# The entry of the feed-forward stages: order of the weight split, the norm's parts and the first tiles

## The chip, the cores and the metric

The kernel runs on one core of one Trainium2 chip. The metric is the device time of one execution, in microseconds (us), as the median of three. The core has TensorE (PE, matmuls; PEld is its weight load), VectorE (DVE), ScalarE (ACT), GpSimd (POOL) and SyncE (SP), which issues most of the transfers. Each engine works through its own list of instructions in program order and waits on semaphores for the others.

## The reference

A block of mixed attention, memory attention and a mixture of experts (two layers) is followed by a second block of two layers, where the change lies. In a layer `l` of the second block, tokens `x` (512 x 1024) and, in layer 0 only, a context `cx` (256 x 1024) go through a mixer and then through a feed-forward stage:

```
h2 = modulate(rms_norm_2(x, norm2_g[l]), sh2, sc2)     # h * (1 + sc2) + sh2
x  = x + g2 * sq_relu_mlp(h2, w_ff1[l], w_ff2[l])      # square(relu(h2 @ w1)) @ w2
# layer 0 only, with the context's own shift, scale and gate:
cx = cx + cg2 * sq_relu_mlp(hc2, w_ff1[l], w_ff2[l])   # w1 1024 x 4096, w2 4096 x 1024
```

Everything is float32.

## The kernel before

Tensors lie transposed: 1024 features as KD = 8 blocks of 128 partitions, tokens along the free dimension, 512 (T) tokens and 256 (CT) of the context side by side. `both` is true in layer 0, where the context is computed too.

**Products in three parts.** In the feed-forward stage a float32 product is made of three faster ones: each operand is split into a rounded high part and the rest, a low part, and high x high + high x low + low x high are summed in one PSUM bank. `tile3` (L713) does that for one output tile of 128 features: for each k of 8 it issues high x high, high x low, low x high, 24 matmuls, waiting for `needs[k]` if given. `joint3` (L687) does it for several tiles at once: all products with the high part of the tokens first (two passes over k, each k of the first waiting for its `needs_high`), then all with the low part (waiting for `needs_low`). It was used so far in the mixer and memory stages of the first block. Banks come from a ring of six (PB).

**Weights.** A block is 1 MB (128 x 2048 values), loaded by SyncE in a fixed order into slots. `split_high` (L1547, ScalarE) waits for the load and rounds the block to its high part, one activation; `split_low` (L2168, VectorE) waits for that and subtracts, one operation. TensorE's `weight_parts` waits for the latter. `ff_chunks` (L388) gives the order of the blocks: ff1 (slab 0, half 0), ff1 (0, 1), ff1 (1, 0), ff1 (1, 1), ff2 (0, 0), and so on. A block of ff1 holds two output tiles, m = 2i and 2i + 1.

**Entry of the stage.** At the end of the mixer stands the differential attention: `df_units(l)` lists its units (16 in layer 1; 24 in layer 0, of which the last four, as four in the middle, are of the context). For each unit ScalarE does two exps and, later, a copy of the turned result; VectorE does two maxima (`df_top`) and one join (`df_join`); TensorE scores, turns and multiplies with the values. A last group of the output projection and the sums of the norm's squares follow on TensorE. Then the engines meet (`meet(("ff", l))`), and:

- ScalarE (L2022 on): `high(0)`, the first block's split; the norm's root (a logarithm and an exp) for the tokens and, in layer 0, the context; `mod_shift` (L1794): the high parts ("hh") of the eight token blocks, then of the context's, each with the shift added.
- VectorE (L2701 on): `low(0)`; `mod_norm` (L2452): for the tokens three Newton steps on the root, then scaled tokens ("h", k) and low parts ("h2", k - 2) in turn; then the same for the context. A high part needs its scaled token, a low part needs its high part.
- TensorE (L1436): for block 0 tile m = 0 of the tokens, the same tile of the context, then m = 1 of both; then the next block.

Then a loop over the blocks: at step n ScalarE first splits block n + 1, then takes the two tiles of block n: relu of the tokens' bank, relu of the context's bank, square of both, rounded copy (hidden, high part). VectorE makes the low part of block n + 1 and then the low parts of the hidden tiles. With `both`, the next layer's conditioning (ada) blocks come between the blocks from step 3 on.

Of the kernel before, what the change touches and what calls it, by code (L numbers as in the profile page):

```python
# [29 lines left out]
ADD, MUL, SUB, MAX = ALU.add, ALU.mult, ALU.subtract, ALU.max  # L30
# [177 lines left out]
class Steps:  # L208
# [9 lines left out]
    def after(self, key):  # L218

        sem, value = self.known[key] if self.known is not None else ("tensor_step", 1)  # L220
        return self.sems[sem], value
# [61 lines left out]
def build(nc, A, known):  # L283

    ctx = ExitStack()
    with ctx:
# [382 lines left out]
        def _(eng):  # L669
# [530 lines left out]
            for l in range(L):  # L1200
# [227 lines left out]
                for n, (kind, s, i) in enumerate(ff_chunks()):  # L1428
                    a = n - 1 - ADA_AT
                    if l == 0 and 0 <= a < 3 * KD:  # L1430
                        ada(1, a // KD, a % KD, PO)
                    if l == 0 and a >= KD + 1 and (a - 1) % KD == 0 and a <= 3 * KD + 1:
                        ada_turn(1, (a - 1) // KD - 1, PO)
                    key = (kind, l, s, i)
                    wh, wl = weight_parts(key)
                    if kind == "ff1":  # L1436
                        for m in range(2 * i, 2 * i + 2):
                            c = slice(P * (m % 2), P * (m % 2) + P)
                            for part, cols, N, tag in parts:
                                tile3(("f1" + part, l, s, m), [(wh[:, k, c], wl[:, k, c]) for k in range(KD)],  # L1440
                                      [(S["HH"][:, k, cols], S["HL"][:, k, cols]) for k in range(KD)], N,
                                      free=(WF(key),) if m % 2 and part == parts[-1][0] else (),
                                      needs=[("h2", (tag, l), k) for k in range(KD)] if (s, m) == (0, 0) else ())
                    else:
                        hid = S["HID"].get((l, s))
                        for m in range(4 * i, 4 * i + 4):
                            c = slice(P * (m % 4), P * (m % 4) + P)
                            for part, cols, N, tag in parts:
                                end = part == parts[-1][0] and m % 4 == 3
                                tile3(("f2" + part, l, s, m), [(wh[:, k, c], wl[:, k, c]) for k in range(4)],  # L1450
                                      [(hid[:, k, cols], hid[:, 4 + k, cols]) for k in range(4)], N,
                                      free=((WF(key),) if end else ()) + ((S["HID"].free((l, s)),) if end and i else ()),
                                      needs=[("hid", l, s, k) for k in range(4)] if m == 0 else ())
                            if s == SLABS - 1 and m >= 2:
                                next_sums([m - 2])
# [5 lines left out]
        def _(eng):  # L1461
# [105 lines left out]
            for l in range(L):  # L1567
# [7 lines left out]
                def high(t):  # L1575
                    eng.wait_ge(*after(("rope", l, t)))
                    act(S["H5R"][:, t, :], S["TA"].get(("g", l, t))).then_inc(*done(("high5", l, t)))
# [235 lines left out]
            for l in range(L):  # L1813
# [174 lines left out]
                def df_roots(j):  # L1988
                    root(("od", l, j), S, PB)
                    if both:  # L1990
                        root(("odc", l, j), S, PB, CT)
# [8 lines left out]
                for i in range(len(us) + DF_LAG + 1):  # L2000
                    if i == len(us) // 2 + DF_POST - 1:
                        df_squares(0)
                    if i == len(us) // 2 + DF_POST:
                        df_roots(0)
                    if i < len(us):
                        df_exp(us[i], 0)
                    if DF_LAG <= i < len(us) + DF_LAG:
                        df_down(us[i - DF_LAG])
                    if i < len(us):
                        df_exp(us[i], 1)  # L2010
                    if DF_LAG < i and df_ends(us[i - DF_LAG - 1]):
                        u = us[i - DF_LAG - 1]
                        shares(df_okey(u), S, u[3] + 1)
# [8 lines left out]
                    split_high((kind, l, s, i))  # L2022

                order = list(ff_chunks())
                high(0)
                root(("n2x", l), S)
                if both:
                    root(("n2c", l), S, n=CT)
# [36 lines left out]
        def _(eng):  # L2065
# [117 lines left out]
            for l in range(L):  # L2183
# [30 lines left out]
                def low(t):  # L2214
                    eng.wait_ge(*after(("high5", l, t)))
                    tt(S["L5R"][:, t, :], S["TA"].get(("g", l, t)), S["H5R"][:, t, :], SUB).then_inc(*done(("low", l, t), S["TA"].free(("g", l, t))))
# [235 lines left out]
            def mod_norm(n, l, S, H, both, parts=None):  # L2452

                for r in range(2 if both else 1):
                    tag = (f"n{n}{'xc'[r]}", l)
                    N = (T, CT)[r]
                    cols = slice(0, T) if r == 0 else slice(T, T + CT)
                    y = rstd(tag, S, PO, N)
                    for k in range(KD + 2):
                        if k < KD:  # L2460
                            stt(H[:, k, cols], (X, C)[r][:, k, :], (G1, G2)[n - 1][l][:, k, r:r + 1], y, MUL, MUL).then_inc(*done(("h", tag, k), *((S["Y"].free(tag),) if k == KD - 1 else ())))
                        if parts and k >= 2:
                            eng.wait_ge(*after(("hh", tag, k - 2)))
                            stt(parts["HL"][:, k - 2, cols], H[:, k - 2, cols], ADA[l][:, 22 + k, r:r + 1], parts["HH"][:, k - 2, cols], ADD, SUB).then_inc(*done(("h2", tag, k - 2)))

            def ada_columns(l, q, ring):
                key = ("adT", l, q)
# [12 lines left out]
            for l in range(L):  # L2480
# [136 lines left out]
                def beside(g):  # L2617
                    return lambda i: add_out(g, range(2 * i - 2, 2 * i)) if 1 <= i <= KD // 2 else None
# [58 lines left out]
                us = df_units(l)  # L2677
                for i in range(len(us) + DF_LAG + 2):
                    beside(1)(i)
                    if i < len(us):  # L2680
                        df_top(us[i], 0)
                    if 1 <= i <= len(us):
                        u = us[i - 1]
                        df_join(u)
                        if df_ends(u):
                            shares(df_okey(u), S, [])
                    if i == len(us) // 2 + DF_POST:
                        df_post(0)
                    if i < len(us):
                        df_top(us[i], 1)  # L2690
                    if DF_LAG + 1 < i and df_ends(us[i - DF_LAG - 2]):
                        u = us[i - DF_LAG - 2]
                        c = int(u[0] == "dc")
                        out_scaled(df_okey(u), S, (T, CT)[c], S["YG"][:, u[2], (slice(0, T), slice(T, T + CT))[c]], ("od2", l, u[2], c))
# [8 lines left out]
                    split_low((kind, l, s, i))  # L2703

                order = list(ff_chunks())
                low(0)
                mod_norm(2, l, S, S["H"], both, S)
                for n, (kind, s, i) in enumerate(order):
                    a = n - 2 - ADA_AT
# [214 lines left out]
```

## Time and profile before

| | us |
|---|---|
| median of 3 runs | 3247.66 (3245.68 to 3249.27) |
| profiled execution | 3246.96 |
| its span, first to last instruction | 3245.3 |
| TensorE busy | 3011.3 |
| VectorE busy | 1348.9 |
| ScalarE busy | 1088.3 |
| mean granted clock of TensorE | 0.970 |

The span is what the timeline covers; times in the rows count from its start. Layer 0's feed-forward stage begins near 1893 us, layer 1's near 2870 us, and the latter runs almost to the end. A row of the timeline gives the start, the duration, engine and line, what is written and read, how many instructions are merged ("x3") and, in brackets, how long the engine had stood before and which engine ended it. "PEclk" is the granted clock of TensorE, 1.00 for 2.4 GHz, 0.50 for 1.2 GHz.

### The profile page before, as it was taken

The numbers are of one execution on the slowest core, as the hardware profiler recorded it, in microseconds if no ns is written. First come the engines' busy times: TensorE is split into PE (matmuls) and PEld (weight loads), VectorE is DVE, ScalarE is ACT, GpSimd is POOL, SyncE is SP. The second block draws the span as 40 slices with busy tenths as digits, with TensorE's granted clock in tenths as the row PEclk, the third lists the DMA queues.
The fourth block names the chain that finished last, engine by engine and source line by source line (L and its number), as shares of the span: only waits on it lengthen the run. The fifth ranks groups of instructions, "written<-read, shape, count | busy, mean of one in ns | idle before, by whom it ended". The sixth has DMA issues, their size and how long they took to land.

```text
span 3245.3 us, 39893 instructions
## 1 busy us (share of the span) xinstructions
PE 3011.3 (93%) x16068; PEld 2129.5 (66%) x16068; DVE 1348.9 (42%) x2127; ACT 1088.3 (34%) x1869; POOL 248.5 (8%) x334
## 2 busy tenths in 40 slices
PE   7999979979999799989999789999999999879998
PEld 5657855446568754446676558887886576658886
DVE  5665432246655422334234653232333341644434
ACT  4555321134654311142122542222222131543332
POOL 0011010000100200010002210000001001200000
PEclk9999989999999899999999989999999999989999
DMA  3011259951013299953211002322321221012221
GB/s 145 27 40 69 89 204 415 417 228 52 14 47 111 91 400 418 415 226 142 79 53 39 1 34 110 125 109 104 130 80 58 105 78 46 14 52 91 104 91 52
DMA packets 61492, 414.20 MB, mean 128 GB/s; under 512 B 6992, under 2 KB 7504, under 8 KB 13696
## 3 DMA queue, kind: packets, MB, share of 16 engines
q1 hardware_dynamic: 55664, 392.59, 30.8%
q0 software_dynamic: 4496, 16.98, 1.6%
q8 instruction: 130, 2.13, 0.3%
q10 hardware_dynamic: 1152, 2.10, 0.2%
q14 instruction: 50, 0.41, 0.0%
HBM read 409.53 MB, written 2.10 MB: 127 GB/s over the span
## 4 chain that ended last, share of the span: by engine, by line
PE 85%; DVE 7%; DMA 3%; ACT 3%; issue 2%; POOL 1%; DVEq 0%; SPq 0%; ACTq 0%; POOLq 0%
PE banks L726 82%; PE banks L727 3%; DVE arena L2068 3%; DMA weight<-in_w_up 3%; ACT arena L1464 2%; DVE arena L2655 1%; DVE weight_part L2172 0%; DVE arena L2347 0%; DVE tokens_low L2068 0%; DVE x L2068 0%; DVE arena L2345 0%; POOL arena L2761 0%; ACT weight_part L1464 0%; DMA mats<-in_k_mats 0%; DVE arena L2119 0%
## 5 line engine op out<-in xcount | busy, mean ns | idle before, releaser
L1464 ACT ACTIVATE arena<-banks 128x512 f32<-128x512 f32 (+4 forms) x528 | 293.5, 560 | 1188.6 <-PE banks L726 1036.8
L726 PE MATMUL banks<-weight,arena 128*64 128x512 f32 (+5 forms) x2808 | 574.4, 527 | 27.1 <-ACT arena L1464 13.0
L726 PEld LDWEIGHTS banks<-weight,arena 128*64 128x64 f32 (+2 forms) x2808 | 268.6, 145 | 296.6 <-issue 262.0
L726 PE MATMUL banks<-hidden,weight_part 128*128 128x512 f32 (+1 forms) x2304 | 446.4, 355 | 0.0
L726 PE MATMUL banks<-arena,weight 128*128 128x512 f32 (+1 forms) x1120 | 422.7, 533 | 20.9 <-DVE arena L2068 10.7
L726 PE MATMUL banks<-tokens_high,weight_part 128*128 128x512 f32 (+1 forms) x1536 | 419.8, 359 | 22.9 <-DVE tokens_low L2068 22.8
L726 PEld LDWEIGHTS banks<-hidden,weight_part 128*128 128x128 f32 x2304 | 381.0, 189 | 70.3 <-issue 3.5
L726 PEld LDWEIGHTS banks<-arena,weight 128*128 128x128 f32 x1120 | 211.3, 193 | 212.5 <-issue 186.0
L726 PEld LDWEIGHTS banks<-tokens_high,weight_part 128*128 128x128 f32 x1536 | 275.7, 191 | 82.1 <-DVE tokens_low L2068 29.5
L726 PE MATMUL banks<-tokens_low,weight_part 128*128 128x512 f32 (+1 forms) x768 | 274.1, 357 | 0.0
L2172 DVE TENSOR_TENSOR weight_part<-weight,weight_part 128x2048 fp32r<-128x2048 f32 x98 | 225.1, 2300 | 86.7 <-ACT weight_part L1464 86.5
L1464 ACT ACTIVATE weight_part<-weight 128x2048 fp32r<-128x2048 f32 x98 | 186.0, 1908 | 172.3 <-DMA weight<-in_w_ff 115.5
L2068 DVE SCALAR_TENSOR_TENSOR x<-banks,arena,x 128x512 f32<-128x512 f32 x192 | 143.4, 750 | 232.7 <-PE banks L726 232.1
L2761 POOL TENSOR_TENSOR arena<-arena 128x512 f32<-128x512 f32 x72 | 87.2, 1212 | 1912.6 <-ACT arena L1464 1641.0
L726 PE MATMUL banks<-arena 128*64 128x128 f32 (+2 forms) x2176 | 223.7, 304 | 8.2 <-DVE arena L2129 2.6
L1464 ACT ACTIVATE arena<-banks,arena 128x512 f32<-128x512 f32 (+2 forms) x264 | 182.5, 696 | 129.2 <-DVE arena L2655 99.1
L727 PE MATMUL banks<-mats,arena 128*128 128x128 f32 x1168 | 170.2, 280 | 52.2 <-ACT arena L1464 23.5
L727 PEld LDWEIGHTS banks<-mats,arena 128*128 128x128 f32 x1168 | 133.1, 143 | 101.8 <-issue 45.2
L2719 DVE TENSOR_TENSOR hidden<-arena,hidden 128x768 fp32r<-128x768 f32 (+1 forms) x64 | 52.8, 826 | 332.8 <-ACT hidden L1464 332.8
L726 PEld LDWEIGHTS banks<-arena 128*64 128x64 f32 (+2 forms) x2176 | 149.1, 146 | 55.7 <-issue 35.0
L1464 ACT ACTIVATE arena<-arena 128x512 f32<-128x512 f32 (+5 forms) x270 | 164.8, 625 | 36.8 <-DVE arena L2068 11.7
L2068 DVE SCALAR_TENSOR_TENSOR arena<-arena 128x512 f32<-128x512 f32 (+7 forms) x223 | 121.1, 552 | 119.8 <-ACT arena L1464 109.8
(198 smaller groups left out, 3208.1 us busy)
## 6 DMA issues: line engine op xcount, KB each, us to landing
weight<-in_w_gate SPq DMA_DIRECT2D x64, 1024.0 KB, 13.6
weight<-in_w_up SPq DMA_DIRECT2D x64, 1024.0 KB, 8.2
weight<-in_w_down SPq DMA_DIRECT2D x64, 1024.0 KB, 10.8
weight<-in_w_ff SPq DMA_DIRECT2D x64, 1024.0 KB, 4.8
weight<-in_ada_w SPq DMA_DIRECT2D x48, 1024.0 KB, 5.1
weight<-in_w_in SPq DMA_DIRECT2D x28, 1024.0 KB, 7.6
weight<-in_w_o SPq DMA_DIRECT2D x8, 1024.0 KB, 4.8
weight<-in_w_mem_kv SPq DMA_DIRECT2D x8, 1024.0 KB, 4.8
```

The source lines that it names most:

```text
L726: mm = lambda o, a, b, first=True, last=True: eng.matmul(o, a, b, start=first, stop=last, skip_group_check=True)
L727: tr = lambda o, a, rows=P: eng.transpose(o, a, mat("ident", rows, rows))
L1464: act = lambda o, i, f=ACT.Copy, **k: eng.activation(o, i, f, **k)
L2068: stt = lambda o, a, s, b, p, q: eng.scalar_tensor_tensor(out=o, in0=a, scalar=s, in1=b, op0=p, op1=q)
L2172: tt(low, raw_of(key), high, SUB).then_inc(*done(("split", key)))
L2655: eng.tensor_reduce(s[:, half:half + 1], PB.get_pair(key)[:, 0:T + CT if u[0] == "d" else CT], AX, MAX, negate=True).then_inc(*done(("nb", ...
L2719: tt(hid[:, 4 + m, 0:N], t[:, 0:N], hid[:, m, 0:N], SUB).then_inc(*done(("hid", l, s, m), S["RT"].free((l, s, m))))
L2761: eng.tensor_tensor(a, a, S["SQ"].get((tag, k))[:, 0:n], ADD).then_inc(*done(S["SQ"].free((tag, k)), *((("summed", tag),) if k == first - ...
```

## The change

Four edits, the first three in both layers:

- `split_high` and `split_low` of the first block stand in the attention's loop: ScalarE's ahead of the last unit's first exp, VectorE's one step later, ahead of the last unit's join. `high(0)` and `low(0)` go.
- `mod_norm` makes all eight scaled tokens first and then all eight low parts, for the tokens and then for the context.
- TensorE takes the first block's two token tiles in one `joint3`.
- In layer 0 the token tiles of the second block come next, then the context's tiles of the first block (a `joint3`), then the context's tiles of the second.

```diff
--- before.py
+++ after.py
@@ -1433,14 +1433,28 @@
                         ada_turn(1, (a - 1) // KD - 1, PO)
                     key = (kind, l, s, i)
                     wh, wl = weight_parts(key)
-                    if kind == "ff1":
+                    if kind == "ff1" and s == 0:
+                        XP, CP = [[(S["HH"][:, k, cols], S["HL"][:, k, cols]) for k in range(KD)] for cols in (slice(0, T), slice(T, T + CT))]
+                        ms = range(2 * i, 2 * i + 2)
+                        if i == 0:
+                            first = wh, wl
+                            joint3([("f1", l, 0, m) for m in ms], [halves(first, m) for m in ms], XP, [range(KD)], T, [("hh", ("n2x", l), k) for k in range(KD)],
+                                   [("h2", ("n2x", l), k) for k in range(KD)], [(), () if both else (WF(key),)])
+                            continue
+                        for m in ms:
+                            tile3(("f1", l, 0, m), halves((wh, wl), m % 2), XP, free=(WF(key),) if m % 2 and not both else ())
+                        if both:
+                            joint3([("f1c", l, 0, m) for m in range(2)], [halves(first, m) for m in range(2)], CP, [range(KD)], CT, [("hh", ("n2c", l), k) for k in range(KD)],
+                                   [("h2", ("n2c", l), k) for k in range(KD)], [(), (WF(("ff1", l, 0, 0)),)])
+                            for m in ms:
+                                tile3(("f1c", l, 0, m), halves((wh, wl), m % 2), CP, CT, free=(WF(key),) if m % 2 else ())
+                    elif kind == "ff1":
                         for m in range(2 * i, 2 * i + 2):
                             c = slice(P * (m % 2), P * (m % 2) + P)
                             for part, cols, N, tag in parts:
                                 tile3(("f1" + part, l, s, m), [(wh[:, k, c], wl[:, k, c]) for k in range(KD)],
                                       [(S["HH"][:, k, cols], S["HL"][:, k, cols]) for k in range(KD)], N,
-                                      free=(WF(key),) if m % 2 and part == parts[-1][0] else (),
-                                      needs=[("h2", (tag, l), k) for k in range(KD)] if (s, m) == (0, 0) else ())
+                                      free=(WF(key),) if m % 2 and part == parts[-1][0] else ())
                     else:
                         hid = S["HID"].get((l, s))
                         for m in range(4 * i, 4 * i + 4):
@@ -2002,6 +2016,8 @@
                         df_squares(0)
                     if i == len(us) // 2 + DF_POST:
                         df_roots(0)
+                    if i == len(us) - 1:
+                        split_high(("ff1", l, 0, 0))
                     if i < len(us):
                         df_exp(us[i], 0)
                     if DF_LAG <= i < len(us) + DF_LAG:
@@ -2022,7 +2038,6 @@
                     split_high((kind, l, s, i))
 
                 order = list(ff_chunks())
-                high(0)
                 root(("n2x", l), S)
                 if both:
                     root(("n2c", l), S, n=CT)
@@ -2456,12 +2471,11 @@
                     N = (T, CT)[r]
                     cols = slice(0, T) if r == 0 else slice(T, T + CT)
                     y = rstd(tag, S, PO, N)
-                    for k in range(KD + 2):
-                        if k < KD:
-                            stt(H[:, k, cols], (X, C)[r][:, k, :], (G1, G2)[n - 1][l][:, k, r:r + 1], y, MUL, MUL).then_inc(*done(("h", tag, k), *((S["Y"].free(tag),) if k == KD - 1 else ())))
-                        if parts and k >= 2:
-                            eng.wait_ge(*after(("hh", tag, k - 2)))
-                            stt(parts["HL"][:, k - 2, cols], H[:, k - 2, cols], ADA[l][:, 22 + k, r:r + 1], parts["HH"][:, k - 2, cols], ADD, SUB).then_inc(*done(("h2", tag, k - 2)))
+                    for k in range(KD):
+                        stt(H[:, k, cols], (X, C)[r][:, k, :], (G1, G2)[n - 1][l][:, k, r:r + 1], y, MUL, MUL).then_inc(*done(("h", tag, k), *((S["Y"].free(tag),) if k == KD - 1 else ())))
+                    for k in range(KD if parts else 0):
+                        eng.wait_ge(*after(("hh", tag, k)))
+                        stt(parts["HL"][:, k, cols], H[:, k, cols], ADA[l][:, 24 + k, r:r + 1], parts["HH"][:, k, cols], ADD, SUB).then_inc(*done(("h2", tag, k)))
 
             def ada_columns(l, q, ring):
                 key = ("adT", l, q)
@@ -2677,6 +2691,8 @@
                 us = df_units(l)
                 for i in range(len(us) + DF_LAG + 2):
                     beside(1)(i)
+                    if i == len(us):
+                        split_low(("ff1", l, 0, 0))
                     if i < len(us):
                         df_top(us[i], 0)
                     if 1 <= i <= len(us):
@@ -2703,7 +2719,6 @@
                     split_low((kind, l, s, i))
 
                 order = list(ff_chunks())
-                low(0)
                 mod_norm(2, l, S, S["H"], both, S)
                 for n, (kind, s, i) in enumerate(order):
                     a = n - 2 - ADA_AT
```

## Rows read from the trace of the kernel before

**Rows 1.** The page's first part: engine, busy us, share of the span, instructions.

```profile
PE 3011.3 (93%) x16068; PEld 2129.5 (66%) x16068; DVE 1348.9 (42%) x2127; ACT 1088.3 (34%) x1869; POOL 248.5 (8%) x334
```

**Rows 2.** Waits of TensorE: us in total, times, longest.

```profile
PE banks L726 <- DVE tokens_low L2068: 22.8, 11, 9.3
```

**Rows 3.** Timeline, feed-forward entry, layer 0: start, us, engine, line, [idle <-releaser].

```profile
1893.45 1.91 ACT L1464 ACTIVATE weight_part<-weight 128x2048 fp32r<-128x2048 f32 x1 [1.64 <-PE banks L726]
...
1895.27 0.67 ACT L1464 ACTIVATE arena<-banks,vec 128x512 f32<-128x512 f32 x1
...
1895.97 0.63 ACT L1464 ACTIVATE arena<-arena 128x512 f32<-128x512 f32 x1
...
1897.70 0.68 DVE L2068 SCALAR_TENSOR_TENSOR arena<-arena 128x512 f32<-128x512 f32 x1
...
1899.87 2.08 DVE L2068 SCALAR_TENSOR_TENSOR arena<-x,arena 128x512 f32<-128x512 f32 x3
...
1900.72 1.99 ACT L1464 ACTIVATE tokens_high<-arena 128x512 fp32r<-128x512 f32 x3 [3.16 <-DVE arena L2068]
...
1902.76 0.77 PE L726 MATMUL banks<-tokens_high,weight_part 128*128 128x512 f32 x1 [9.34 <-DVE tokens_low L2068]
...
1919.47 2.29 DVE L2172 TENSOR_TENSOR weight_part<-weight,weight_part 128x2048 fp32r<-128x2048 f32 x1 [1.20 <-ACT weight_part L1464]
```

**Rows 4.** Same entry: stretch, us, busy PE PEld DVE ACT POOL, PEclk, DMA, GB/s.

```profile
1902.70:1906.50 3.80, 3.74 (x9) 2.51 (x9) 3.80 (x6) 1.99 (x4) 0.00 (x0) 0.50 0.02 4
...
1911.60:1913.60 2.00, 0.05 (x1) 0.00 (x0) 1.96 (x6) 1.23 (x3) 0.00 (x0) 1.00 0.00 0
...
1924.30:1927.10 2.80, 2.80 (x25) 2.80 (x24) 0.00 (x0) 0.60 (x1) 0.00 (x0) 1.00 0.00 0
...
1927.10:1943.80 16.70, 16.70 (x98) 14.78 (x97) 4.21 (x3) 7.16 (x9) 0.00 (x0) 1.00 0.18 64
```

**Rows 5.** Timeline, feed-forward entry of layer 1.

```profile
2869.94 1.91 ACT L1464 ACTIVATE weight_part<-weight 128x2048 fp32r<-128x2048 f32 x1 [1.76 <-PE banks L726]
...
2879.25 0.76 PE L726 MATMUL banks<-tokens_high,weight_part 128*128 128x512 f32 x1 [9.35 <-DVE tokens_low L2068]
...
2893.61 0.60 ACT L1464 ACTIVATE arena<-banks 128x512 f32<-128x512 f32 x1 [3.51 <-PE banks L726]
```

**Rows 6.** Timeline, end of differential attention, layer 0.

```profile
1853.93 0.47 ACT L1464 ACTIVATE arena<-banks,arena 128x256 f32<-128x256 f32 x1 [0.41 <-DVE arena L2655]
...
1855.78 0.16 DVE L2661 RECIPROCAL arena<-arena 128x1 f32<-128x1 f32 x1
...
1856.78 0.44 PE L727 MATMUL banks<-mats,arena 128*128 128x128 f32 x2 [0.95 <-DVE arena L2068]
```

**Rows 7.** Timeline, end of differential attention, layer 1.

```profile
2831.26 0.90 ACT L1464 ACTIVATE arena<-banks,arena 128x768 f32<-128x768 f32 x1 [2.49 <-DVE arena L2655]
...
2834.53 0.16 DVE L2661 RECIPROCAL arena<-arena 128x1 f32<-128x1 f32 x1 [1.06 <-ACT arena L1464]
...
2836.05 0.87 PE L727 MATMUL banks<-mats,arena 128*128 128x128 f32 x6 [1.07 <-DVE arena L2068]
```

**Rows 8.** Timeline, last part of the joint pass of the first stage.

```profile
37.46 3.79 PE L726 MATMUL banks<-mix_low,weight_part 128*128 128x512 f32 x16
```

**Rows 9.** Timeline, ScalarE and VectorE inside a block of layer 0.

```profile
1927.39 0.39 ACT L1464 ACTIVATE arena<-banks 128x256 f32<-128x256 f32 x1 [2.33 <-PE banks L726]
...
1929.44 1.90 ACT L1464 ACTIVATE weight_part<-weight 128x2048 fp32r<-128x2048 f32 x1
```

**Rows 10.** Stretches around two gaps of layer 1's attention and output projection.

```profile
2821.50:2824.50 3.00, 0.03 (x1) 0.00 (x0) 2.86 (x7) 1.97 (x4) 0.00 (x0) 1.00 0.03 5
...
2824.70:2828.00 3.30, 3.30 (x18) 2.67 (x20) 2.08 (x3) 0.23 (x1) 0.00 (x0) 0.50 0.00 0
...
2850.10:2855.30 5.20, 5.18 (x6) 2.17 (x7) 0.75 (x1) 0.56 (x1) 0.00 (x0) 0.50 0.00 0
```

**Rows 11.** Timeline of SyncE's queue, layer 1's first feed-forward block.

```profile
2705.73 0.33 SPq L665 DMA_DIRECT2D weight<-in_w_ff  x1
```

## The prediction

> **What bounds the kernel now.** I read the page's head first. TensorE is busy 93% of the span [rows 1], so only a gap on TensorE, or a stretch in which its clock is low, can give time back. The waits of TensorE come next: its waits for the feed-forward low parts are 22.8 us in 11 places, the longest 9.3 [rows 2]. They all lie in the two entries, so I read the timeline there, first layer [rows 3] and second [rows 5], the stretches of the first with clock [rows 4], and last the end of the attention, where the split is put [rows 6, 7].
>
> Entry of layer 0 [rows 3]: TensorE ends the sums at 1893.4; ScalarE splits the block (1.91 us) and only then takes the root; VectorE makes the block's low part (2.29 us, as that of the second block at 1919.47), then the Newton steps from 1897.70, the first scaled token from 1899.87; TensorE starts at 1902.76, after 9.34 us. From 1897.70 to 1918.27 VectorE works through tokens and context without a gap (20.57 us; the row at 1919.47 shows it idle for 1.20 before). Layer 1 is the same with tokens only [rows 5]: first matmul 2879.25.
>
> **Step 1, the split ahead of the norm.** The root now starts where the split started, at 1893.45. Its two activations take 1.33 us (1895.27 to 1895.97 + 0.63), VectorE follows 0.11 later as between these engines elsewhere, so Newton starts at 1894.89 instead of 1897.70: -2.8 us. What is late next is this chain itself, root, Newton, first token. The order is the same in layer 1, again -2.8. The weight block is there long before: in layer 1 its transfer is issued at 2705.7, 125 us ahead of the attention's last unit [rows 11].
>
> What it costs where it goes. Layer 1: ScalarE is idle for 2.49 us ahead of the last unit's first exp [rows 7], which hides 1.91. VectorE's part is put ahead of the last unit's join: VectorE is free 1.06 us before that join, at 2833.47, so the part runs to 2835.7, the join starts there instead of at 2834.53, and TensorE at 2836.05 waits for the join. +1.15 us. Layer 0: the last units are of the context and small, ScalarE is free only from 1853.5; its split runs to 1855.4 and holds up the exps behind it by 1.5 us at most. VectorE's low part takes the join's place, about 1855.7 to 1857.9; the join was at 1855.78, and TensorE at 1856.78 waits for it [rows 6]. +2.1 us. Behind this join everything up to the output projection is one chain, so both prices are paid in full. Bounds: 0, if another wait covers it, and 2.3, the whole instruction.
>
> **Step 2, scaled tokens ahead of low parts, joint passes.** (Times here and in steps 3 and 4 are without the attention's 2.1 and 1.15.) The first high part starts 0.85 us behind the first scaled token (1900.72 against 1899.87, [rows 3]) and takes 0.72; with the token now at 1897.06 it ends at 1898.63; TensorE starts 0.14 later, at 1898.77, 3.99 us earlier than 1902.76. High parts follow every 0.665 us (three scaled tokens take 2.08), the last at 1903.3; low parts follow, done at 1897.06 + 16 x 0.665 = 1907.7. The joint pass has 48 matmuls. At full clock one takes 0.2275 us, as in the joint pass of the first stage, 16 in 3.79 us [rows 8]; at the low clock 0.427. The clock is at its lower level (1.2 GHz, granted 0.50) for 3.8 us after the start of before [rows 4] and 3.5 in layer 1; with 3.7, 8.7 matmuls run in it and 39.3 x 0.2275 = 8.95 us follow: 12.65 us in all, and neither high nor low parts are later than their matmul. Both tiles are done at 1911.4 in layer 0 and 2875.26 + 12.65 = 2887.9 in layer 1.
>
> Layer 1: before, the second block's first matmul comes 0.28 ahead of the activation at 2893.61 [rows 5], 2893.33. Its parts are ready in time: VectorE is through with the tokens 1898.77 to 1907.7 = 8.9 us after the first matmul and with the block 2.3 later, 11.2 against 12.65. So it starts at 2887.9: -5.4 us, and later stages are TensorE-bound. Bounds: -4.7 (low clock for 5.2 us, as at 2850.10 in [rows 10], half of the 1.5 us more lost) and -7.2 (full clock throughout).
>
> **Step 3, layer 0: the second block comes late.** The context's tokens stand before the second block in both queues, and TensorE now asks for that block behind the two token tiles of the first, no longer behind their context tiles too. VectorE's 20.57 us run from 1894.89 to 1915.46, the block's low part to 1917.75, TensorE goes on at 1917.85. It stood from 1911.4: 6.4 us, a new gap, against the one of 2.0 at 1911.60 [rows 4] that goes, and 9.34 that becomes 5.4.
>
> The Trainium skill ("TensorE: Matmul & The Clock Gate", section "Step-by-step: what each phase is for") says that only weight loads are pulled ahead and matmuls stay in program order. That speaks against the change: the context's tiles 0 and 1, whose block is there, can't slip into this gap. If they could, the third block would start 9 us sooner than before and the total be near 3235.5; nothing in the trace of before shows matmuls passing each other.
>
> Then: 48 matmuls of the second block's token tiles, 10.9; the low clock after such a gap lasted 3.5 to 5.2 us in four places (3.8 and 5.2, the first and the last, in [rows 4, 10]), each half lost, 1.75 to 2.6, I take 2.1; two context tiles, 2.88 each ([rows 4]: 25 matmuls in 2.80), 5.76. They end at T = 1936.6.
>
> **Step 4, context last.** ScalarE's loop is in the old order: for tile 0 tokens, context, square of both, hidden. So it stands at the context of tile 0 until T, and the split of the third block is behind both tiles. From the context's activation to the next split is 2.05 us [rows 9]; tile 1 needs that and one activation more, 2.7; the split starts at T + 4.9, VectorE's part ends at T + 9.1 (1.90 [rows 9] and 2.29 behind it), TensorE starts the third block at T + 9.2. It has two context tiles meanwhile, 5.85 with a short wait for a bank: a gap of 3.35 us. Third block: 1936.6 + 9.2 = 1945.8, before 1943.8 [rows 4]: +2.0. A gap of 3.06 us at 2821.5 was followed by 3.3 us at the low clock, one of 2.0 at 1911.60 by none [rows 10, 4]; 3.35 is nearest to the first, so half of 3.3, +1.65, bounds 0 and 2.6. After that both queues have 16.7 us a block [rows 4] for about 8 us of ScalarE's work, so nothing is handed on. The first block's slot is freed about 9 us later, and the load that waits for it is for a block used more than 30 us later.
>
> **Sum.** Layer 0: 2.1 + 2.0 + 1.65 = +5.75. Layer 1: 1.15 - 5.4 = -4.25. Net +1.5 us. The profiled execution took 3246.96 (span 3245.3 and 1.7 around it), so 3248.5; it lies 0.7 below the median of the three, 3247.66, and the spread of those is 3.6. I say 3248.4.
>
> **Rivals.** A: the second block is not late in layer 0, because ScalarE or VectorE reaches its split before the context. Then 48 + 48 token matmuls and four context tiles follow 1898.77 without a gap: 12.65 + 10.9 + 11.5 = 35.1, third block at 1933.9, -9.9; with +2.1 and -4.25 that is 3234.9. For it: in layer 1, with no context before it, the block is ready 1.4 us early. Against, for layer 0: the code's order in both queues, and VectorE's 20.57 us without a gap in [rows 3].
> B: the gaps are there, but the clock stays high in both (one of 2.0 us did so): -2.1 and -1.65, 3244.7. Against: all gaps above 3 us that I read had a low stretch behind them.
> C, the other side: the clock stays low longer, 5.2 us as at 2850.10, after each of four restarts (two joint passes 0.75 each, first gap 0.5, second 0.95): 3251.4, slower than before. It decides from about 4 us of low clock on in each. For it: two of the stretches read were this long.
> The Trainium skill (same page, "What's actually happening") says that the number of matmuls at the low clock after a start varies from run to run. By it B and C are chance, not kernel, and a few us between executions remain whatever the change does; the 3.6 us spread here agrees.
> D: the change doesn't do what it says, the high parts don't lead: TensorE would start with the first low part, now behind eight tokens. That is excluded by the wait on each high part alone.
>
> **How the numbers follow.** Forecast 0.57, A 0.07, B 0.17, C 0.19. The likeliest case gives 3248.4, by its own bounds 3245 to 3251. The range 3242.5 to 3254 takes in B and C with the spread of runs, and leaves A and unforeseen waits outside. 0.2% is 6.5 us: only A and an unforeseen gain lie under 3241.2, 0.09; over 3254.2 lies C with another wait, 0.06; the rest, 0.85, is no change that can be told.
>
> **What would show it.** In the changed profile: in both layers the first feed-forward matmul 5.4 us behind the last of the sums, not 9.3; the last join of each attention behind a 2.29 us instruction of VectorE; in layer 0 a gap of about 6.4 us ended by VectorE's low part of the block after the first 48 matmuls, another of about 3.4 after four context tiles, in layer 1 none; third block of layer 0 some 4 to 6 us later than before, last stage shorter by 4. Wrong: no gap in front of the second block in layer 0 (then A), or a join in the attention that is not late (then up to 3.3 us less).

## The result and the profile after

The changed kernel takes 3253.82 us in the median of 20 runs (3248.10 to 3258.92), the kernel before 3249.53 in 20 runs beside it (3245.68 to 3253.67): ratio 1.0014, 95% interval 1.0008 to 1.0020, so 4.5 us slower (2.6 to 6.5). That is within the 0.2% I had called no change, but over 20 runs it is clear, and it is three times the 1.5 us of my sum. The forecast time, 3248.4, also stood on a single execution (3246.96), 2.6 us below the median of the 20. The profiled span is 3250.6 us.

The first part of the page and TensorE's waits of the changed kernel (us in total, times, longest) answer to [rows 1, 2]: the waits for low parts are gone, and two new pairs stand in their place.

```profile
PE 3020.0 (93%) x16068; PEld 2137.8 (66%) x16068; DVE 1348.6 (41%) x2127; ACT 1086.6 (33%) x1869; POOL 248.5 (8%) x334
```

```profile
PE banks L726 <- ACT tokens_high L1478: 10.9, 2, 5.5
...
PE banks L726 <- DVE weight_part L2187: 9.1, 2, 5.9
```

The timeline of the changed kernel, end of the attention and entry of layer 0, answers to [rows 6, 3]:

```profile
1853.37 1.90 ACT L1478 ACTIVATE weight_part<-weight 128x2048 fp32r<-128x2048 f32 x1
...
1855.66 2.29 DVE L2187 TENSOR_TENSOR weight_part<-weight,weight_part 128x2048 fp32r<-128x2048 f32 x1
...
1857.87 0.16 DVE L2675 RECIPROCAL arena<-arena 128x1 f32<-128x1 f32 x1
...
1858.85 0.57 PE L727 MATMUL banks<-mats,arena 128*128 128x128 f32 x2 [1.99 <-DVE arena L2083]
...
1897.37 0.69 ACT L1478 ACTIVATE arena<-banks,vec 128x512 f32<-128x512 f32 x1 [1.65 <-PE banks L726]
...
1898.86 0.69 DVE L2083 SCALAR_TENSOR_TENSOR arena<-arena 128x512 f32<-128x512 f32 x1 [3.58 <-ACT arena L1478]
...
1901.03 5.39 DVE L2083 SCALAR_TENSOR_TENSOR arena<-x,arena 128x512 f32<-128x512 f32 x8
...
1902.75 9.44 PE L726 MATMUL banks<-tokens_high,weight_part 128*128 128x512 f32 x32 [5.42 <-ACT tokens_high L1478]
```

VectorE's low part stands ahead of the join, 2.09 us later than at 1855.78, and TensorE turns 2.07 later. Behind it the root begins at once, Newton 1.49 later, eight tokens in a row, and TensorE starts 5.42 us behind the sums instead of 9.34. What follows in layer 0, on the three engines:

```profile
1912.03 3.79 PE L726 MATMUL banks<-tokens_low,weight_part 128*128 128x512 f32 x16
...
1916.74 1.90 ACT L1478 ACTIVATE weight_part<-weight 128x2048 fp32r<-128x2048 f32 x1
...
1919.36 2.29 DVE L2187 TENSOR_TENSOR weight_part<-weight,weight_part 128x2048 fp32r<-128x2048 f32 x1
...
1921.70 0.79 PE L726 MATMUL banks<-tokens_high,weight_part 128*128 128x512 f32 x1 [5.88 <-DVE weight_part L2187]
...
1941.20 0.39 ACT L1478 ACTIVATE arena<-banks 128x256 f32<-128x256 f32 x1 [22.08 <-PE banks L726]
...
1945.91 1.90 ACT L1478 ACTIVATE weight_part<-weight 128x2048 fp32r<-128x2048 f32 x1
...
1947.84 2.29 DVE L2187 TENSOR_TENSOR weight_part<-weight,weight_part 128x2048 fp32r<-128x2048 f32 x1 [0.84 <-ACT weight_part L1478]
...
1950.18 0.50 PE L726 MATMUL banks<-tokens_high,weight_part 128*128 128x512 f32 x1 [3.17 <-DVE weight_part L2187]
```

The joint pass is done at about 1915.8. The second block's low part comes behind all context tokens, a gap of 5.88. ScalarE's next row is at 1941.20: it waited 22.08 us for the context of tile 0, and the third block is split after both tiles; a gap of 3.17. The stretches of TensorE there (the last three columns are granted clock, DMA share, GB/s):

```profile
1921.70:1927.20 5.50, 5.50 (x13) 4.34 (x14) 0.00 (x0) 0.00 (x0) 0.00 (x0) 0.50 0.00 0
...
1947.10:1950.10 3.00, 0.00 (x0) 0.00 (x0) 2.27 (x1) 2.90 (x5) 0.00 (x0) 1.00 0.58 210
...
1951.20:1954.60 3.40, 3.40 (x9) 2.67 (x8) 1.20 (x2) 3.34 (x4) 0.00 (x0) 0.50 0.00 0
```

The clock was low for the 5.5 us behind the first gap, still full in the second and low for 3.4 us soon after it. Layer 1, answering to [rows 7, 5], has no such gaps:

```profile
2842.83 0.15 DVE L2675 RECIPROCAL arena<-arena 128x1 f32<-128x1 f32 x1
...
2844.35 0.88 PE L727 MATMUL banks<-mats,arena 128*128 128x128 f32 x6 [2.11 <-DVE arena L2083]
...
2859.78 17.04 PE L726 MATMUL banks<-arena,weight 128*128 128x512 f32 x32 [4.68 <-DVE arena L2083]
...
2880.11 0.69 ACT L1478 ACTIVATE arena<-banks,vec 128x512 f32<-128x512 f32 x1 [1.85 <-PE banks L726]
...
2885.49 9.54 PE L726 MATMUL banks<-tokens_high,weight_part 128*128 128x512 f32 x32 [5.50 <-ACT tokens_high L1478]
...
2898.50 0.39 PE L726 MATMUL banks<-tokens_high,weight_part 128*128 128x512 f32 x1
```

From the first high part (2885.49) to the second block (2898.50) are 13.0 us, where the old order took 14.2. But from the last join to the projection it takes 16.95 us, before 15.58.

### The profile page after: what moved, and what is told of

The parts are those of the page before. It is cut to its first block, busy times and chain, and to the rows that moved or that the text cites. A ratio compares the mean times of both kernels' runs of the same rounds, so it can differ in the third digit from the quotient of the medians.

```text
span 3250.6 us, 39897 instructions
## 1 busy us (share of the span) xinstructions
PE 3020.0 (93%) x16068; PEld 2137.8 (66%) x16068; DVE 1348.6 (41%) x2127; ACT 1086.6 (33%) x1869; POOL 248.5 (8%) x334
## 4 chain that ended last, share of the span: by engine, by line
PE 85%; DVE 7%; DMA 3%; ACT 3%; issue 2%; POOL 1%; DVEq 0%; SPq 0%; ACTq 0%; POOLq 0%
PE banks L726 82%; PE banks L727 3%; DMA weight<-in_w_up 2%; DVE arena L2083 2%; ACT arena L1478 2%; DVE arena L2669 1%; DVE weight_part L2187 1%; DVE arena L2362 0%; DVE x L2083 0%; DVE arena L2360 0%; POOL arena L2776 0%; DVE tokens_low L2083 0%; DMA mats<-in_k_mats 0%; ACT weight_part L1478 0%; DVE arena L2134 0%
## 5 line engine op out<-in xcount | busy, mean ns | idle before, releaser
L726 PE MATMUL banks<-tokens_low,weight_part 128*128 128x512 f32 (+1 forms) x768 | 266.8, 357 | 0.0
L2187 DVE TENSOR_TENSOR weight_part<-weight,weight_part 128x2048 fp32r<-128x2048 f32 x98 | 225.1, 2301 | 76.3 <-ACT weight_part L1478 76.1
```

The source lines that it names most:

```text
L726: mm = lambda o, a, b, first=True, last=True: eng.matmul(o, a, b, start=first, stop=last, skip_group_check=True)
L2187: tt(low, raw_of(key), high, SUB).then_inc(*done(("split", key)))
```

## The experiments

Each kernel ran beside the kernel before. Their profiles are compared in stretches counted from a row of their own, so that a shift earlier in the execution drops out: in each attention, from the last scores to the last join and from there to the projection; in each entry, from the end of the sums to the first matmul of the fifth block (the first that reads the hidden tiles). The projection itself and its sums are not in the table. All in us, from the timelines of one profile each; before_again and after_again are one execution each, so they have no ratio.

| kernel | attention 0 | attention 1 | entry 0 | entry 1 | ratio (95%) |
|---|---|---|---|---|---|
| before | 1.7 + 11.8 | 3.2 + 15.6 | 86.0 | 56.2 | |
| before_again | 1.7 + 13.7 | 3.2 + 15.6 | 86.0 | 56.2 | |
| after | 3.8 + 13.8 | 4.2 + 17.0 | 90.2 | 51.1 | 1.0014 (1.0008-1.0020) |
| after_again | 3.8 + 14.1 | 4.2 + 17.0 | 90.5 | 51.2 | |
| e_split_only | 3.8 + 13.8 | 4.2 + 16.9 | 84.0 | 53.5 | 0.9997 (0.9988-1.0006) |
| e_split_early | 1.7 + 12.8 | 3.2 + 14.6 | 90.2 | 50.7 | 1.0005 (0.9996-1.0014) |
| e_filler | 3.8 + 11.9 | 4.2 + 13.9 | 90.5 | 51.1 | 1.0001 (0.9992-1.0009) |
| e_in_projection | 1.7 + 12.7 | 3.2 + 15.8 | 90.1 | 51.2 | 1.0009 (1.0000-1.0018) |
| e_between | 1.5 + 13.9 | 3.2 + 15.7 | 90.1 | 50.9 | 0.9992 (0.9984-1.0001) |
| e_no_joint | 3.8 + 13.9 | 4.2 + 16.9 | 87.6 | 55.2 | 1.0022 (1.0013-1.0031) |
| e_context_second | 3.8 + 13.9 | 4.2 + 16.9 | 76.7 | 51.2 | 0.9974 (0.9964-0.9983) |
| e_both_ahead | 3.8 + 13.9 | 4.2 + 16.9 | 76.3 | 52.0 | 0.9972 (0.9963-0.9982) |
| e_best | 1.7 + 12.7 | 3.2 + 15.7 | 76.3 | 51.3 | 0.9972 (0.9962-0.9983) |
| e_best2 | 1.7 + 13.8 | 3.2 + 15.7 | 76.4 | 50.9 | 0.9951 (0.9937-0.9965) |

### The two kernels again

> The kernel before, unchanged, for a second profile of the attention's end. Theory: last join to projection again near 11.8 and 15.6 us, low clock 7 and 10 us there. Rival (chance): 12.7 or more in layer 0, up to the 13.8 and 17.0 of the changed kernel.

> The changed kernel, unchanged, for a second profile. Theory: 13.8 and 16.9 us again, low clock 17 and 20 us, as in all four kernels so far that have the split at the last join and no filler. Rival (chance): one of them under 13 or 16.

The stretches from the last join to the projection, kernel before, second profile:

```profile
1856.57:1870.30 13.73, 5.53 (x24) 3.00 (x23) 5.90 (x13) 4.08 (x9) 0.00 (x0) 0.54 0.00 1
...
2836.91:2852.40 15.49, 6.57 (x58) 4.97 (x53) 5.03 (x9) 4.02 (x6) 0.00 (x0) 0.73 0.00 1
```

Changed kernel, first profile:

```profile
1857.87:1871.70 13.83, 5.48 (x23) 3.02 (x23) 5.89 (x14) 3.95 (x8) 0.00 (x0) 0.54 0.00 1
...
2842.83:2859.70 16.87, 7.48 (x48) 5.30 (x48) 5.03 (x10) 3.35 (x5) 0.00 (x0) 0.58 0.00 1
```

In layer 1 both theories hold: 15.6 at a granted clock of 0.73 in either profile of before, 17.0 at 0.58 in either of after, and 16.9 to 17.0 in all six profiles with that join late and no filler. That is no chance. The timelines say where it goes. TensorE turns the joined tile 1.52 us behind the join and then waits three more times up to the projection. These three waits come to 7.93 us or within 0.01 of it in 13 of the 14 profiles (8.02 in e_in_projection): the whole difference between 15.6 and 17.0 is in the time of its own matmuls. In before_again the clock was back at full from 2844.20 to 2847.60, 7.3 us behind the join; in the changed kernel it stayed low from 2845.40, 2.6 us behind the join, up to the projection:

```profile
2844.20:2847.60 3.40, 1.20 (x6) 0.30 (x2) 0.69 (x1) 1.23 (x2) 0.00 (x0) 1.00 0.00 0
...
2845.40:2859.70 14.30, 6.61 (x42) 4.66 (x42) 3.52 (x5) 3.28 (x5) 0.00 (x0) 0.50 0.00 1
```

In layer 0 one profile can't tell: the kernel before itself took 11.8 in one (clock 0.92) and 13.7 in the other (0.54). The seven profiles without a late join lie between 11.8 and 13.9, 13.1 in the mean, the six with it and no filler between 13.8 and 14.1. So some tenths of a us may be the change's there too, but my theory of 1.8 us, formed on one profile of each, falls.

### The split alone

```diff
+ split_high / split_low of block 0 at the attention's end
- high(0) / low(0) at the entry
  (norm and tiles as before)
```

> The kernel before with the split moved alone: both instructions of the first block at the end of the attention, norm and tiles in the old order. Theory (the moved split delays the last join by 2.1 and 0.9 us, and the longer wait makes TensorE's clock fall sooner or stay low longer up to the output projection, 1.8 and 1.9 us more): +6.7 in the attentions, -5.6 in the entries, 1.1 us slower than before, within 0.1%. Rival (the added low clock of the changed kernel was chance): 3.0 - 5.6, 2.6 us faster. In both the first feed-forward matmul comes 6.5 us behind the last of the sums, not 9.3.

Measured 0.9997 (0.9988 to 1.0006), -1.0 us with 2.9 to either side: the time excludes neither. The profile does more: the attentions show 17.7 and 21.2 us as in the changed kernel, the entries 2.0 and 2.7 us less than before. The entry of layer 0 with the split ahead and nothing else is thus 84.0, and the rest of the change makes 90.2 of it.

### A filler in the wait

```diff
+ if u == us[-1]:
+     o = PB.take(("filler", l))          # spare bank (its wait and release left out here)
+     for _ in range(2): mm(o, mat("ident"), mats[:, 0:T])
  eng.wait_ge(*after(("p", u)))           # the last join
```

> The changed kernel with two extra float32 matmuls of 512 columns (about 1.7 us of TensorE) on a spare bank, ahead of TensorE's wait for the last join of each attention; their result is read by nobody. Theory: the late join stays late by 2.1 and 0.9, but the clock stays at 1.00 behind it, the low stretch gets shorter by one or two of the 3.4 us seen, 1 to 3.5 us less than the changed kernel. Rival (chance, or the low clock costs nothing in a chain bound by the other engines): no change or 1 us slower than the changed kernel.

The join is as late as in the changed kernel (3.8, 4.2), but behind it:

```profile
1861.48:1873.30 11.82, 4.00 (x25) 1.84 (x23) 5.90 (x14) 3.95 (x8) 0.00 (x0) 0.95 0.00 1
...
2845.61:2859.40 13.79, 5.72 (x52) 3.38 (x50) 5.02 (x10) 3.35 (x5) 0.00 (x0) 0.84 0.00 1
```

The mean clock is 0.95 and 0.84, and the same work takes 11.9 and 13.9 us, 2.0 and 3.1 less than in the changed kernel; in layer 1 it is even 1.7 below the kernel before. The 2.0 of layer 0 lie within what the kernel before shows by itself (11.8 and 13.7) and prove nothing; the 3.1 of layer 1 are outside of all that was seen there (14.6 to 17.0), with the same 7.93 us of waits. The ratio, 1.0001 against 1.0014, says 4.2 us less than the changed kernel, a little above the 1 to 3.5 expected. So a low clock in this chain does cost time, though TensorE is busy for less than half of it.

### Other places for the split

```diff
e_split_early:    at units len(us) - 9 / - 8 (layer 0), - 5 / - 4 (layer 1)
e_in_projection:  ScalarE between the squares of tiles 1 and 2, VectorE behind sum 2
e_between:        ScalarE ahead of mod_squares, VectorE ahead of add_out(3)
```

> The changed kernel with the first block split four to nine units earlier, where ScalarE and VectorE stand idle for over 2 us in each unit. Theory: the attention ends as in the kernel before, low clock included, and the entries keep their gain: 6.7 us less than the changed kernel, 1.6 us faster than before. Rival (low clock by chance): only the 3.0 of the two joins come back, 2.1 us slower than before. Second rival (the split itself costs wherever it stands): no change against the changed kernel, 5 us slower than before.

> The changed kernel with the first block's split moved once more, into the last group of the output projection: ScalarE's between the squares of tiles 1 and 2, VectorE's behind tile 2 of the sums. Theory (the split costs where it stands in the attention, whose units are one chain through three engines, and there it costs once more through the clock): in the projection TensorE is the bound, so the attention ends as before, 11.8 and 15.6 us from the last join to the projection (13.8 and 17.0 in the changed kernel), the entry keeps its gain: 6.7 us less than the changed kernel, 1.6 us faster than before. Rival (a split that is late for nobody still costs, as four to nine units earlier it did): no change against the changed kernel.

> The changed kernel with the first block's split between attention and output projection: ScalarE's ahead of the first square, VectorE's ahead of the first sum, where the kernel before shows them idle for 8 and 4 us. Theory: nothing waits for either there; last join, projection and sums as in the kernel before, against the changed kernel 6.6 us less from the last scores to the projection, the entries as in the changed kernel: 1.5 us faster than before. Rival (the chain's longer low clock is there without the late join too, as 13.7 us against 6.8 in layer 0 when the split stood in the projection): 4 to 5 us less than the changed kernel, within 1 us of before.

Early was no gift: from the first score to the last, layer 0 took 119.2 us and layer 1 84.8, against 115.0 to 116.3 and 82.8 before, so it paid about 3 to 4 and 2 us there. What it won at the end (3.2 and 3.5 against the changed kernel) it had mostly spent before. 1.0005 is 1.6 us slower than before (1.3 faster to 4.6 slower): nearest to the first rival's 2.1, but not for its reason, as behind the join layer 1 took 14.6 us, less than before; theory (1.6 faster) and second rival (5 slower) are both half right.

In the projection the split missed its forecast: 1.0009 is 2.9 us slower than before, where 1.6 faster was expected and the rival said 5 slower. Layer 1's attention was as before, and layer 0's within the spread above, but layer 1's root began 22.3 us behind the projection's start instead of 20.3:

```profile
2865.51 2.29 DVE L2187 TENSOR_TENSOR weight_part<-weight,weight_part 128x2048 fp32r<-128x2048 f32 x1 [0.78 <-ACT weight_part L1478]
...
2866.14 2.80 POOL L2776 TENSOR_TENSOR arena<-arena 128x512 f32<-128x512 f32 x1 [1.04 <-ACT arena L1478]
...
2874.62 3.68 PE L726 MATMUL banks<-arena,mats 128*128 128x512 f32 x4 [2.10 <-POOL arena L2776]
```

GpSimd adds up the squares there, 1.27 us each. The one that starts while VectorE makes the block's low part takes 2.80. The Trainium skill ("SBUF — State Buffer", section "Who interferes with whom") has this: a VectorE instruction with both inputs in SBUF and a GpSimd instruction that reads SBUF lock each other out, the second waits for the first to end. The row agrees: 2865.51 + 2.29 + 1.27 is 2869.07, it ended at 2868.94. With the squares held up as well, the sums wait 2.10 us for GpSimd, 1.20 in the changed kernel. That is the smaller part. The four matmuls of the sums then take 3.68 us at a granted clock of 0.54, where the changed kernel took 1.98 at full clock, 1.7 of the 2.0 us:

```profile
2874.60:2878.30 3.70, 3.68 (x4) 1.12 (x4) 0.00 (x0) 0.00 (x0) 0.00 (x0) 0.54 0.56 235
```

e_best shows the same 3.68. That the longer wait made the clock fall is likely, but no run isolates it.

Between attention and projection it costs nothing that a row shows: attention 15.4 and 18.9, in before_again 15.4 and 18.8, entries 90.1 and 50.9. The intervals give 4.8 us less than the changed kernel; the ratio, 0.9992 against 1.0014, says 7, with 3 to either side of its own. Against before it is 2.6 us faster (5.2 faster to 0.3 slower): the expected 1.5 lies in that, and the rival (within 1 us of before) isn't excluded.

### The joint pass

```diff
- joint3(tiles 0 and 1)
+ tile3(tile 0, needs low parts); tile3(tile 1)
```

> The changed kernel with the first two token tiles one after the other, each waiting for low parts, instead of the joint pass. Theory: the first matmul now waits for the first low part behind eight tokens, 4.5 us later than in the changed kernel; layer 1 pays about 4 us, in layer 0 the gap before the second block swallows it. 4 us slower than the changed kernel, 9 us slower than before, ratio 1.0025. Rival (the joint pass gives little, VectorE's order is the gain): within 1 us of the changed kernel.

```profile
1908.49 0.76 PE L726 MATMUL banks<-tokens_high,weight_part 128*128 128x512 f32 x1 [9.90 <-DVE tokens_low L2084]
```

Layer 1 pays 4.1 us, as said: behind eight scaled tokens TensorE starts 10.0 us after the sums instead of 5.5 (the row is that of layer 0). Layer 0 gains 2.6, which I had not expected: its matmuls end so late that the gap before the second block is 1.96 and the clock stays full after it. 1.0022 against 1.0014: +2.6 us, intervals +1.5, between the 4 expected and the rival's 1.

### The order of layer 0

```diff
e_context_second:
+ joint3(context tiles of block 0)   # directly behind its token tiles
  tile3(token tiles of block 1)
- joint3(context tiles of block 0)
```

> The changed kernel with one part undone in layer 0: the context's tiles of the first block stand directly behind its token tiles, the second block's tiles behind them in the new order. Theory (context last makes both gaps): the context's tiles fill most of the 5.9 us, the third block is split in time, no gap of 3.2 and no low clock behind it; the third block starts about 11.7 us sooner than in the changed kernel, 6 us faster than before, ratio 0.998. Rival (the second block's split itself is the bound and the gap only moves): the gap of 5.9 stays, only the second goes, 3 to 4 us less than the changed kernel, 1 us slower than before.

TensorE's waits in the entry of that kernel:

```profile
PE banks L726 <- ACT tokens_high L1479: 5.4, 1, 5.4
...
PE banks L726 <- DVE weight_part L2188: 0.2, 1, 0.2
```

The rival fails: one edit undone takes both gaps away but for 0.2 us, and entry 0 goes from 90.2 to 76.7. The 8.5 us less than before are more than the 6 expected.

```diff
e_both_ahead:
  ScalarE: high parts of tokens; + high(1); high parts of the context; + high(2); loop
  VectorE: norm of tokens;       + low(1);  norm of the context;       + low(2);  loop
```

> The changed kernel with, in layer 0, the second weight block split between tokens and context on ScalarE and VectorE, and the third ahead of ScalarE's wait for the first context tile. Theory: both gaps (5.9 and 3.2 us) and the low clock behind them go, the third block starts 12.4 us sooner and 1.0 of low clock goes with it: 8.3 us faster than before, ratio 0.9974. Rival (the context's tokens get late instead, as they now stand behind the block): a gap of some us in front of the first context tile, 3 to 5 us faster than before.

```profile
1906.01 1.90 ACT L1478 ACTIVATE weight_part<-weight 128x2048 fp32r<-128x2048 f32 x1
...
1910.57 2.28 DVE L2191 TENSOR_TENSOR weight_part<-weight,weight_part 128x2048 fp32r<-128x2048 f32 x1
...
1917.87 1.90 ACT L1478 ACTIVATE weight_part<-weight 128x2048 fp32r<-128x2048 f32 x1
...
1920.48 2.28 DVE L2191 TENSOR_TENSOR weight_part<-weight,weight_part 128x2048 fp32r<-128x2048 f32 x1
```

VectorE has the second block ready at 1912.85, two us before the joint pass ends, and TensorE's waits from there to 1960 are empty. 76.3, a second way to the same 14 us, and 9 us faster than before (8.3 expected). The context's tokens are ready in time.

### Both together

> The version the runs point to: the changed kernel with the first block split in the output projection, the second between tokens and context, the third ahead of ScalarE's wait for the context. Theory: the sum of the parts, 8.3 us faster than before by the last two and 6.7 by the first, 15 us faster, ratio 0.9954. Rival (the parts overlap, since TensorE's clock falls in the entry anyway): as with the last two alone, ratio 0.9972.

> The same place of the first split, together with the second block split between tokens and context and the third ahead of the wait for the context. Theory: 2.0 us less than with the split in the projection, where it held up layer 1's squares and GpSimd; against before -9.8 in layer 0's entry, -5.1 in layer 1's: about 14 us faster, ratio 0.9957. Rival (as before: placing the split gives nothing that the clock doesn't take back): ratio 0.9972.

e_best took 0.9972, no better than e_both_ahead; that is the rival's number. Layer 1 took 2.3 us less than there in the attention, but 22.3 against 18.5 from the projection's start to the end of the sums. The profiles still leave 2.4 us of gain, most of it in layer 0's attention; the ratios, 3 us wide to either side, can't tell. e_best2 has the split between attention and projection: 3233.86 us in the median, ratio 0.9951 (0.9937 to 0.9965), 16 us faster than before and 20 than the changed kernel, the forecast 14. Against before its entries took 9.6 us less in layer 0 and 5.3 less in layer 1.

## Why the prediction was wrong

The sum was +1.5 us, measured +4.5. Against before_again, the profile with the like clock in layer 0, the terms are:

- **Step 1, gain.** Right: in either layer the root starts 1.8 us sooner behind the sums and Newton 1.0 sooner behind the root, 2.8 in all; e_split_only, which has nothing else, shows 2.7 in entry 1.
- **Step 1, price at the join.** Right in place and size: +2.1 and +1.05 (said 2.1 and 1.15).
- **Step 1, "both prices are paid in full".** This is the step that failed, in layer 1. The delay of the join is not all that is paid: with 1.05 us more of waiting TensorE's clock is low almost throughout (0.58 for 0.73), and the same work takes 1.4 us longer up to the projection and 0.4 from its start to the end of the sums (20.2 for 19.8), with every wait in between unchanged. I booked 1.15 and gave 2.3 as the upper bound; it is 2.85. I had weighed the clock behind the two new gaps of step 3 and 4, not behind the wait that step 1 adds. In layer 0 the same stretch took from 11.8 to 13.9 without any late join, so nothing of it is shown to be the change's.
- **Step 2.** Right: TensorE 3.93 us earlier (said 3.99), the joint pass 13.0 us (said 12.65), entry 1 -5.0 (said -5.4).
- **Step 3.** Right: a gap of 5.9 (said 6.4) behind the first 48 matmuls, ended by the block's low part. The low clock behind it lasted 5.5 us, 2.8 lost instead of 2.1.
- **Step 4.** Right: gap 3.17 (said 3.35), third block 52.85 us behind the sums, before 50.4: +2.4 (said 2.0); low clock 3.4 us, as at [rows 10]: 1.7 (said 1.65). Entry 0 in all +4.2 (said 3.65).

Terms (attention 0, entry 0, attention 1, its projection, entry 1): 2.2 + 4.2 + 2.4 + 0.4 - 5.0 = 4.2, measured 4.5 (2.6 to 6.5). Said: 5.75 - 4.25 = 1.5. Of the 2.7 between the two sums layer 1's clock is 1.7; the rest is entries 0 (0.5) and 1 (0.4) and 0.1 in attention 0, all to one side. With the other profile of before the first term would be 4.2: that this sum comes so near is in part the choice of the profile with the like clock. Rival C ended nearest (3251.4), with its mechanism, a longer low clock, but in another place. That matmuls stay in program order was borne out: TensorE stood for 5.88 us with the context's tiles of the first block in its list right behind the two token tiles it waited for, and e_context_second, where they come first and wait for nothing, shows that all they read is ready at that time; its time is 3239.8, where "if they could pass" gave 3235.5.

Open: why layer 0's stretch takes 11.8 or 13.8 from one execution to the next. That the late join causes layer 1's 1.4 us through the clock rests on the unchanged waits, on the filler, and on the spread over the kernels: 15.6 to 15.8 without a late join, 16.9 to 17.0 with it. e_split_early, with the join in time, took 14.6, so what TensorE does before the join counts too.

## What to carry to other kernels

That an engine has a gap does not make work moved there free: something stands behind it in each place, and in a chain over three engines with TensorE waiting, 1.05 us of delay cost 1.8 more through the clock. Moving independent tiles last also moves their consumer's place in another engine's queue: check for every queue what now stands behind the moved wait. The best place found here was where both engines are idle and TensorE is about to have a long run of its own (e_between, e_best2).

## What the hardware showed

The clock's low stretches vary between executions of one kernel (after the last join of layer 0: mean 0.92 in one, 0.54 in the other, 2 us apart), so one profile of each kernel doesn't tell a 2 us effect there. Two matmuls put into the wait of layer 1's attention were worth 3.1 us behind them, by the profiles. There a wait of TensorE for the join of 0.20, 1.06 or 2.11 us went with 13.9, 15.6 to 15.8 (14.6 with the early split) or 17.0 us from the join to the projection, the difference all in TensorE's own matmuls. GpSimd's 1.27 us sum took 2.80 beside a VectorE subtraction of 2.29.
